# A streaming encoder step: input, first pooling and MLP as one block, banded products in high and low parts

## The reference

```python
    for gi, win in enumerate(POOL_WINDOWS):          # 2, 4, 8, 16
        cs = slice(gi * POOL_GW, (gi + 1) * POOL_GW)
        lo = csum[:, POOL_HIST + 1 - win:POOL_HIST + 1 - win + T, cs]
        cnt = jnp.minimum(t + 1 + n_hist, win).astype(jnp.float32)[None, :, None]
        groups.append((hi[..., cs] - lo) / cnt)
    pooled = jnp.concatenate(groups, axis=-1) - h.astype(jnp.float32)
    mixed = jnp.einsum('btgc,gcd->btgd', pooled.reshape(B, T, POOL_GROUPS, POOL_GW), w.astype(jnp.float32))
    out = mixed.reshape(B, T, D) * scale.astype(jnp.float32)
```

## Time and profile before

| | us |
|---|---|
| median of 3 runs (1389.69 to 1393.47) | 1390.83 |
| the profiled execution, its own time | 1393.68 |
| its span | 1391.9 |
| PE busy (share of the span) | 1290.7 (93%) |
| DVE busy | 809.7 (58%) |
| ACT busy | 507.8 (36%) |
| POOL busy | 71.9 (5%) |

### The profile page before, as it was taken

How to read it: one execution, slowest core, us unless ns; L and a number is a source line. 1 busy time by engine, 2 the same in 40 slices (tenths; PEclk the granted TensorE clock), 3 DMA queues, 4 the chain that set the end, 5 groups by cost and what they waited for, 6 DMA issues and landing times. The chain is left out here.

```text
span 1391.9 us, 25166 instructions
## 1 busy us (share of the span) xinstructions
PE 1290.7 (93%) x11244; PEld 1232.4 (89%) x11244; DVE 809.7 (58%) x838; ACT 507.8 (36%) x547; POOL 71.9 (5%) x55
## 2 busy tenths in 40 slices
PE   5999999999799999986998697899999989999998
PEld 4999999876699999986877596699999989999997
DVE  4557533677646664349668673656664355666333
ACT  4433322532443433232453323343433244334232
POOL 3100000100000000000003200001000012000000
PEclk9999999997699999997999796899999999999998
DMA  6254545523024545453431000054545542445430
GB/s 213 95 178 154 173 160 166 178 75 102 31 91 155 178 152 179 154 158 100 127 108 61 8 9 6 9 160 154 179 152 177 188 139 86 162 153 179 153 121 34
DMA packets 99033, 175.92 MB, mean 126 GB/s; under 512 B 11504, under 2 KB 18824, under 8 KB 98942
## 3 DMA queue, kind: packets, MB, share of 16 engines
q1 hardware_dynamic: 98620, 174.45, 38.2%
q10 hardware_dynamic: 322, 0.10, 0.0%
HBM read 172.21 MB, written 2.33 MB: 125 GB/s over the span
## 5 line engine op out<-in xcount | busy, mean ns | idle before, releaser
L323 DVE TENSOR_TENSOR w_lo<-raw,w_hi 128x2048 fp32r<-128x2048 f32 (+1 forms) x104 | 238.2, 2291 | 296.2 <-ACT w_hi L309 295.9
L309 ACT ACTIVATE w_hi<-raw 128x2048 fp32r<-128x2048 f32 (+1 forms) x104 | 197.6, 1901 | 326.6 <-PE PS L340 325.5
L338 PE MATMUL PS<-mlp_x_hi,w_hi 128*128 128x288 f32 x1024 | 305.0, 298 | 4.9 <-PEq L981 3.4
L338 PE MATMUL PS<-ff_hi,w_hi 128*128 128x288 f32 x1024 | 303.1, 296 | 0.0
L339 PE MATMUL PS<-mlp_x_hi,w_lo 128*128 128x288 f32 x1024 | 302.1, 295 | 0.0
L339 PE MATMUL PS<-ff_hi,w_lo 128*128 128x288 f32 x1024 | 302.1, 295 | 0.0
L340 PE MATMUL PS<-mlp_x_lo,w_hi 128*128 128x288 f32 x1024 | 301.1, 294 | 0.0
L340 PE MATMUL PS<-ff_lo,w_hi 128*128 128x288 f32 x1024 | 301.1, 294 | 0.0
L338 PEld LDWEIGHTS PS<-mlp_x_hi,w_hi 128*128 128x128 f32 x1024 | 191.9, 187 | 7.3 <-issue 3.8
L340 PEld LDWEIGHTS PS<-ff_lo,w_hi 128*128 128x128 f32 x1024 | 192.8, 188 | 0.0
L340 PEld LDWEIGHTS PS<-mlp_x_lo,w_hi 128*128 128x128 f32 x1024 | 192.8, 188 | 0.0
(11 more groups left out here) (454 smaller groups left out, 1495.4 us busy)
## 6 DMA issues: line engine op xcount, KB each, us to landing
raw<-in_w_up SPq DMA_DIRECT2D x64, 1024.0 KB, 5.3
raw<-in_w_down SPq DMA_DIRECT2D x64, 1024.0 KB, 5.0
raw<-in_attn_w_in SPq DMA_DIRECT2D x6, 1024.0 KB, 5.6
raw<-in_attn_w_out SPq DMA_DIRECT2D x4, 1024.0 KB, 5.2
raw<-in_rwkv_w_r SPq DMA_DIRECT2D x4, 1024.0 KB, 5.0
raw<-in_rwkv_w_k SPq DMA_DIRECT2D x4, 1024.0 KB, 5.8
raw<-in_rwkv_w_v SPq DMA_DIRECT2D x4, 1024.0 KB, 5.5
raw<-in_rwkv_w_o SPq DMA_DIRECT2D x4, 1024.0 KB, 5.3
```

The source lines that it names most:

```text
L309: nc.scalar.activation(w_hi[:, n % SPLITS, :, 0:width], raw[:, n % RAWS, :, 0:width], ACT.Copy) \
L323: nc.vector.tensor_tensor(w_lo[:, n % SPLITS, :, 0:width], raw[:, n % RAWS, :, 0:width], w_hi[:, n % SPLITS, :, 0:width].bitcast(F32), ALU ...
L338: nc.tensor.matmul(out, hi, rhs_hi(k), start=first and k == 0, stop=False)
```

## The change

Three things are done.

1. The input stage is no longer a block; its parts stand at the head of the block of `pool0` and `mlp0` (`input_parts`). `x_prompt` is loaded in two halves of its columns. The history comes first and is turned first on PE. The constant band is loaded last, behind the four raw weight chunks. `vecs` is turned together with tile 3. Each tile's square is made when the tile arrives; splits of the first four tiles come behind the pool weights' split, and the copies of the last four tiles alternate with low parts of the first four.
2. In both poolings the tail products and the state products are cut in two. Those of the first pair stand ahead of the second pair's projections, the others behind the sums of squares.
3. The bands are made in fp32r. `pool_mixed` is evicted twice: ACT makes the high part of all six pieces and DVE the low part of all six. The band is rounded to fp32r by ACT (`band_hi`). A low part, `band_lo`, is made for the first 16 columns only. The 15-column product becomes 16 columns wide.

```diff
-BAND = 2 * P + HIST + DEC
+BAND = 2 * P + 16 + DEC
 LAST = DEC + HIST
+FIRST = 16
 HEADS, DH = 8, 128
 IHEADS, DI = 8, 64
...
+            act.wait_ge(S["pre_hi"].sem, S["pre_hi"].at(HALF))
+            pool_tail_hi(act, 0)
...
+            dve.wait_ge(S["pre_lo"].sem, S["pre_lo"].at(HALF))
+            pool_tail_lo(dve, 0)
...
+        f = slice(HALF * half, HALF * half + HALF)
+        nc.scalar.activation(tail_r[:, f, 0:DEC], x_hi[:, f, SEQ:T].bitcast(F32), ACT.Copy).then_inc(S["tail_hi"].sem, 1)
+
+    def pool_tail_lo(dve, half):
+        f = slice(HALF * half, HALF * half + HALF)
+        nc.vector.tensor_copy(tail_rest[:, f, 0:DEC], x_lo[:, f, SEQ:T].bitcast(F32)).then_inc(S["tail_lo"].sem, 1)
...
+        def sp(sp):
+            sp.dma_start(fixed[:, :], consts[:, 0:3 * P]).then_inc(const_s.sem, 16)
+            sp.dma_start(pool_history[0:HIST, :], A["state_pool"][0, 0]).then_inc(S["pool_hist_in"].sem, 16)
+            for q, sig in enumerate((x_s, late_s)):
+                f = slice(512 * q, 512 * q + 512)
+                sp.dma_start(x_tok[:, 0:2, f], A["x_prompt"][0][:, f].rearrange("(t p) d -> p t d", p=P)) \
+                    .then_inc(sig.sem, 16)
+                if q == 0:
+                    sp.dma_start(x_tok[0:DEC, 2, :], A["x_sample"][0]).then_inc(x_s.sem, 16)
+            pool_load_weights(sp, 0)
+            first_loads(sp)
+            pool_load_band(sp)
...
+            for c in range(C):
+                if c == KT:
+                    pe.wait_ge(late_s.sem, late_s.at(16))
+                if c == VEC_TILE:
+                    pe.wait_ge(S["hist_lo"].sem, S["hist_lo"].at(1))
+                    pe.wait_ge(S["load2"].sem, S["load2"].at(16 * (len(VEC_SOURCES) + 1)))
+                    rest = NVEC * C - P
+                    nc.tensor.transpose(PS[:, c, VEC_AT:VEC_AT + P], rows[:, 0, :], ident)
+                    nc.tensor.transpose(PS[:, c, VEC_AT + P:VEC_AT + P + rest], rows[0:rest, 1, :],
+                                        ident[0:rest, 0:rest])
+                for t, (t0, n) in enumerate(TOK_TILES):
+                    mm = nc.tensor.transpose(PS[:, c, t0:t0 + n], x_tok[0:n, t, c * P:(c + 1) * P], ident[0:n, 0:n])
+                mm.then_inc(pe_s.sem, 1)
+
+        def dve(dve, c):
+            dve.wait_ge(pe_s.sem, pe_s.at(c + 1))
+            if c == VEC_TILE:
+                nc.vector.tensor_copy(vecs[:, :], PS[:, c, VEC_AT:VEC_AT + NVEC * C]).then_inc(vec_s.sem, 1)
...
+        band = at(f"pool_band_hi{j}", unit(7), [P, len(WINDOWS), BAND], F32R)
+        band_lo = at(f"pool_band_lo{j}", unit(8), [P, len(WINDOWS), FIRST], F32R)
         diag = at(f"gain_diag{j}", unit(6), [P, C, P])
         rows = at(f"pool_rows{j}", unit(0), [P, 512])
         pool_hi, pool_lo, sums, rms, root, turned, hist_hi, z, z_act, z_dve, pooled, moved, rows_pe, rows_out, made = (
...
+        def act(act):
+            if halved:
+                history_hi(act)
+                split_hi(act, stage, left, pool_hi)
+                square_tiles(act, left, S["pool_sq"])
+            else:
+                arrive["act"](act)
+                history_hi(act)
+                for half in range(2):
+                    tiles = range(HALF * half, HALF * half + HALF)
+                    for c in tiles:
+                        act.wait_ge(arrived.sem, arrived.at(c + 1))
+                        square_tiles(act, (c,), S["pool_sq"])
+                        if half:
+                            split_hi(act, stage, (c,), pool_hi)
+                    if not half:
+                        pool_weights_hi(act)
+                        act.wait_ge(S["vecs_in"].sem, S["vecs_in"].at(1))
+                        split_hi(act, stage, tiles, pool_hi)
+                        act.wait_ge(pool_hi.sem, pool_hi.at(HALF))
+                        pool_tail_hi(act, 0)
             act.wait_ge(pool_hi.sem, pool_hi.at(len(left)))
-            nc.scalar.activation(tail_r[:, :, 0:DEC], x_hi[:, :, SEQ:T].bitcast(F32), ACT.Copy) \
-                .then_inc(S["tail_hi"].sem, 1)
+            pool_tail_hi(act, 1)
             make_hi(act, a, early=True)
+            act.wait_ge(S["pool_band_in"].sem, S["pool_band_in"].at(16))
+            nc.scalar.activation(band[:, :, :], pool_band[:, :, :], ACT.Copy).then_inc(S["band_hi"].sem, 1)
...
             nc.scalar.activation(rstd[:, 0:2], var[:, 0:2], ACT.Sqrt).then_inc(root.sem, 1)
             nc.scalar.activation(rstd[0:DEC, 2:3], var[0:DEC, 2:3], ACT.Sqrt).then_inc(root.sem, 1)
...
+            for pair in range(2):
+                for k, (tile, n) in enumerate(((0, P), (1, P), (2, LAST))):
+                    if tile == 2:
+                        act.wait_ge(made.sem, made.at(1))
+                    act.wait_ge(z.sem, z.at(ORDER[pair][k]))
+                    nc.scalar.activation(mixed[0:n, tile, 512 * pair:512 * pair + 512], PS[0:n, 4 * pair + tile, :],
+                                         ACT.Copy, scale=rstd[0:n, tile:tile + 1]).then_inc(z_act.sem, 1)
+            act.wait_ge(rows_pe.sem, rows_pe.at(2))
             nc.scalar.activation(rows[:, :], PS[:, 7, :], ACT.Copy, scale=rstd[:, 3:4]).then_inc(rows_out.sem, 1)
...
+            else:
+                history_lo(dve)
+                for c in range(HALF):
+                    arrive["dve"](dve, c)
+                pool_weights_lo(dve)
+                for c in range(HALF):
+                    arrive["dve"](dve, HALF + c)
+                    first_lo(dve, c)
+                dve.wait_ge(pool_lo.sem, pool_lo.at(HALF))
+                pool_tail_lo(dve, 0)
+                for c in range(HALF, C):
+                    first_lo(dve, c)
             dve.wait_ge(pool_lo.sem, pool_lo.at(len(left)))
-            nc.vector.tensor_copy(tail_rest[:, :, 0:DEC], x_lo[:, :, SEQ:T].bitcast(F32)) \
-                .then_inc(S["tail_lo"].sem, 1)
+            pool_tail_lo(dve, 1)
             make_lo(dve, a, early=True)
+            dve.wait_ge(S["band_hi"].sem, S["band_hi"].at(1))
+            nc.vector.tensor_tensor(band_lo[:, :, :], pool_band[:, :, 0:FIRST], band[:, :, 0:FIRST].bitcast(F32),
+                                    ALU.subtract).then_inc(S["band_lo"].sem, 1)
             make_lo(dve, a + 1, early=True)
             dve.wait_ge(sums.sem, sums.at(1))
             dve_own.step(dve, nc.vector.tensor_scalar(var[:, 0:4], PS[:, 3, 0:4], 1.0 / D, EPS, ALU.mult, ALU.add))
             nc.vector.reciprocal(var[:, 0:4], var[:, 0:4]).then_inc(rms.sem, 1)
-            dve.wait_ge(root.sem, root.at(2))
...
+            for pair in range(2):
+                for tile, n in ((0, P), (1, P), (2, LAST)):
+                    out = slice(512 * pair, 512 * pair + 512)
+                    dve.wait_ge(z_act.sem, z_act.at(3 * pair + tile + 1))
+                    nc.vector.scalar_tensor_tensor(mixed_lo[0:n, tile, out], PS[0:n, 4 * pair + tile, :],
+                                                   rstd[0:n, tile:tile + 1], mixed[0:n, tile, out].bitcast(F32),
+                                                   ALU.mult, ALU.subtract).then_inc(z_dve.sem, 1)
...
+        def state_rows_of(pe, q):
+            for c in range(KT * q, KT * q + KT):
+                mm = nc.tensor.matmul(PS[64 * q:64 * q + 64, 7, c % KT * P:(c % KT + 1) * P], X[:, c, ROWS:T],
+                                      diag[:, c, :], start=True, stop=True)
+            mm.then_inc(rows_pe.sem, 1)
...
+        def tail_product(pe, pair):
+            pe.wait_ge(S["hist_lo"].sem, S["hist_lo"].at(1))
+            pe.wait_ge(S["tail_hi"].sem, S["tail_hi"].at(pair + 1))
+            pe.wait_ge(S["tail_lo"].sem, S["tail_lo"].at(pair + 1))
+            pool_project(pe, pair, 2)
 
         def pe(pe):
             if not halved:
-                pool_turn_history(pe)
+                arrive["pe"](pe)
                 pe.wait_ge(S["pool_w_lo"].sem, S["pool_w_lo"].at(1))
                 pe.wait_ge(pool_lo.sem, pool_lo.at(HALF))
                 pool_project(pe, 0, 0)
                 pool_project(pe, 0, 1)
+            tail_product(pe, 0)
+            pe.wait_ge(made.sem, made.at(1))
+            state_rows_of(pe, 0)
...
+            tail_product(pe, 1)
+            state_rows_of(pe, 1)
+            pe.wait_ge(S["band_lo"].sem, S["band_lo"].at(1))
             pe.wait_ge(rms.sem, rms.at(1))
...
+                for part, src in enumerate((mixed, mixed_lo)):
+                    nc.tensor.matmul(PS[:, c, P:SEQ], src[:, 1, f], band[:, g, P + FIRST:2 * P + FIRST],
+                                     start=part == 0, stop=False)
+                for src in (mixed, mixed_lo):
+                    nc.tensor.matmul(PS[:, c, 0:P], src[:, 0, f], band[:, g, 0:P], start=False, stop=False)
+                    nc.tensor.matmul(PS[:, c, P:P + FIRST], src[:, 0, f], band[:, g, P:P + FIRST], start=False, stop=False)
+                nc.tensor.matmul(PS[:, c, 0:FIRST], mixed[:, 0, f], band_lo[:, g, :], start=False, stop=False)
```

(23 more changed lines are left out.)

175 lines of the change are left out of this document (63 added, 112 removed).

## The result

The changed kernel took 1405.95 us (4 runs, 1404.87 to 1406.46) against 1390.37 us before (4 runs): ratio 1.0098, 95% interval 1.0076 to 1.012. It is 15.6 us slower; the forecast was 4.3 us faster, and 1405.95 lies outside the range. The profiled execution took 1406.46 us, its span is 1404.7 us. The profiled execution of before was 3.3 us over its median, so the two spans differ by 12.8 us only.

What follows compares the result with a forecast made beforehand. PE was taken to wait for DVE's low parts and POOL's sums of squares. First pooling -5.2, second -0.7 and bands +1.6 made -4.3 us: 1386.5 on the median's scale, range 1382 to 1395 (the forecast's own 1383.5 to 1389).

Steps and rivals of the forecast that it cites:

- the bands' term of the sum: Bands of both poolings: nine fp32r products and two row changes cost 0.10 us more per tile, +1.6 us for 16 tiles.
- 11 x 0.11 = 1.21 per tile: Bands: nine single-record fp32r products and two changes of rows, each priced at 0.11 us, since stationary load sets the cost.
- Rival A: Bands: short fp32r products cost 0.22 each, a tile 2.2 us, total 1402.4; milder form 1393.6; chance 0.20.
- Rival C: First pooling: PE stays at the lower clock throughout, 31 products cost 0.10 more each, total 1389.6 us; chance 0.11.
- first pooling, start of the bands: Input and first pooling: bands start at 35.2 instead of 40.37 us, 5.2 earlier.
- second pooling, start of the bands: Second pooling: bands start at 1158.75 against 1159.46 us, 0.7 earlier.
- First projection at 19.6: First pooling: PE starts projections when DVE's low parts of X are ready, 19.6 instead of 21.72 us, 2.1 earlier.
- 12.0 us from there to `var`: First pooling: 10.1 us of products, 0.75 of state products and 1.1 of sums of squares, giving `var` at 31.6.
- The 3.0 us wait for POOL in the first pooling goes: First pooling: POOL's adds end at about 24.5, PE asks at 30.5; the wait and the clock's fall behind it go.
- `var` to bands 3.65: New eviction chain: 0.83 to first eviction, 2.07 for ACT's three high parts, 0.74 for DVE's last low part.
- The sums of POOL were to set `var`: Second pooling: POOL's sums stay at 1153.6 us and `var` at 1155.1, despite PE's earlier tail and state products.
- Rival B: Bands priced by columns: a tile falls to 0.57 us, -8.6 for 16 tiles, total 1376.3; chance 0.08.

Runs made afterwards that it cites:

- the rest alone: Changed kernel with fp32 bands and single evictions as before, keeping merged input and PE's new order: 1385.42 us, ratio 0.9938; repeated, 1389.74 us, ratio 0.9977.

## Why the prediction was wrong

The step that failed is the bands' term of the sum, "16 tiles: +1.6 us". Its price, "11 x 0.11 = 1.21 per tile", is right at the upper clock: 1.17 to 1.20 measured. But the sum multiplied it by 16, as if the clock held. It held for three tiles of sixteen, and the others took 1.88 to 2.13. So the term measured +13.15 us, and the MLP's starts, which the sum did not have, +3.3. The experiments show why: nine short fp32r products a tile lose the clock with no wait ahead, and in the second pooling the wait of the new eviction chain is enough for it. Rival A forecast a tile of 2.2 us and 1402.4, close to what came, but by another mechanism: it said that each product costs 0.22 from the first on; they cost 0.08 to 0.19 until the clock fell. Rival C had the clock, but only before the bands. That the bands themselves could lose it was no rival at all, although showed a fall to 0.50 behind a wait and the prediction had the price of the lower level (0.22 for 0.12).

Term by term, in us, of the two profiled executions:

| term | forecast | measured |
|---|---|---|
| first pooling, start of the bands | -5.2 | -2.0 |
| second pooling, start of the bands | -0.7 | -1.5 |
| 16 band tiles | +1.6 | +13.15 |
| start of the MLP, twice | none | +3.3 |
| the rest | none | -0.1 |
| sum | -4.3 | +12.8 |

Point by point:

- First projection at 19.6: 22.53, wrong by 2.9. The sum had tile 3 of X at 11.2; it came at 13.41 for want of the vectors (11.49), whose landing the prediction did not ask about. The pool weights' low part took 2.88 instead of 2.5.
- 12.0 us from there to `var`: 12.05 (22.53 to 34.58). Right, with some luck. The 29 slow products were taken over from before; from the first projection to the sums it is 9.7 to 11.1 us in the seven profiles with this order, and in the two of the rest alone, at 11.08 and 9.69, the clock rises at 28.6 and at 25.4.
- The 3.0 us wait for POOL in the first pooling goes: right, in every kernel with the merged input. In the second pooling the rest alone got a new one of 1.86.
- `var` to bands 3.65: 3.75 and 3.74. Right. A wait of 1 to 2 us in both poolings: 1.25 in the first, 2.50 in the second, which is outside.
- First bands at 35.2: 38.33, and 2.9 of these 3.1 us are the first point.
- Second pooling. The sums of POOL were to set `var`; they did not, since its three additions took 3.33 us and not 5.23. PE kept the upper clock and came to the sums 10.6 us after its first projection, not 12.7. DVE's low part of the weights then stood ahead of `var` (1155.70 to 1157.99), while PE had started the last of its sums at 1156.32. So PE's gain became a wait of 2.5 us. From the first projection to the bands it is 1.5 us less than before, against the 0.7 forecast. The pooling as a whole, up to the MLP, was to keep its length within 0.5 us and is 6.6 us longer.
- Rival B: gone. No tile took less than 1.17 us, and a product of 16 columns costs 0.08 where one of 128 costs 0.11 or 0.14, far from an eighth.
- The chances, as they are split up, add up to 0.45 faster and 0.45 same, not 0.46 and 0.44. Nothing hangs on it.

## What to carry to other kernels

A price per product taken at the upper clock holds only if the granted clock holds through the new stream, and a busy PE does not ensure that: 17 products in 2 us read as 2.00 busy in the stream of short ones (the clock fell) and in that with four of seven 256 columns wide (it did not). Before replacing a few fp32 products by many short fp32r ones, ask whether they can be made fewer and wider, even with zeros. And where a change takes cover from a chain of evictions, count the wait twice: for itself, and for the clock of what follows. In all nine sets of bands in which the clock fell, or in the wait ahead of which it fell, it stayed at 1.2 GHz to their end, and came back 2.5 to 5.0 us into the MLP.
